# Order of the two column chunks of every expert: 2048 then 1536 columns, or 1536 then 2048

## What is computed

```python
D_MODEL = 1024; D_FF = 7 * D_MODEL // 2      # 3584
def swiglu(x, wg, wu, wd):
    return (jax.nn.silu(x @ wg) * (x @ wu)) @ wd

logits = (xt @ w_router).astype(jnp.float32)
top_v, top_i = lax.top_k(logits, TOP_K)      # 2 of 8
w = jax.nn.softmax(top_v, axis=-1)
gates = jnp.sum(jax.nn.one_hot(top_i, N_EXPERTS) * w[..., None], axis=1)
for e in range(N_EXPERTS):
    y = y + gates[:, e:e + 1] * swiglu(xt, wg[e], wu[e], wd[e])
```

## Time and profile before

| | us |
|---|---|
| median of 3 runs | 1382.66 (1381.82 to 1394.2) |
| profiled execution, its own time | 1382.52 |
| its span, first to last instruction | 1380.8 |
| TensorE busy | 1329.7 (96%) |
| VectorE, ScalarE, GpSimd busy | 746.8, 643.1, 35.4 |

### The profile page before, as it was taken

The page is one execution under the profiler, slowest core; times in us unless marked ns, Lnnn a source line. Parts: engine busy times, 40 slices in busy tenths (PEclk is TensorE's granted clock), DMA queues, the critical chain, the costliest instruction groups (busy, mean ns, idle before and its releaser), DMA issues.

```text
span 1380.8 us, 16480 instructions
## 1 busy us (share of the span) xinstructions
PE 1329.7 (96%) x6528; PEld 947.1 (69%) x6528; DVE 746.8 (54%) x787; ACT 643.1 (47%) x751; POOL 35.4 (3%) x96
## 2 busy tenths in 40 slices
PE   7999999999999999999999999999989999989994
PEld 6877788888878777658468558478448568538561
DVE  4646644445455567547358357268247358327443
ACT  5465433444354646347157147157137147236341
POOL 2000000000000000000000000000000000000001
PEclk9999999999999999999999999999999999999998
DMA  9730855554535459899999999999999999999995
GB/s 334 252 138 1 305 183 185 189 194 164 183 101 179 153 209 347 321 421 388 418 422 421 421 420 419 417 421 422 422 420 418 419 420 422 422 421 418 419 419 226
DMA packets 102031, 444.38 MB, mean 322 GB/s; under 512 B 9982, under 2 KB 22140, under 8 KB 71228
## 3 DMA queue, kind: packets, MB, share of 16 engines
q1 hardware_dynamic: 100388, 438.24, 80.5%
q0 software_dynamic: 1440, 4.98, 0.9%
q10 hardware_dynamic: 120, 0.04, 0.0%
HBM read 439.30 MB, written 3.93 MB: 321 GB/s over the span
## 4 chain that ended last, share of the span: by engine, by line
PE 85%; DMA 6%; ACT 4%; DVE 3%; issue 1%; POOL 0%; DVEq 0%; POOLq 0%; ACTq 0%; SPq 0%
PE bank L915 81%; PE bank L918 3%; DMA part_in<-in_moe_w_down_dram 2%; DMA more<-in_moe_w_down_dram 2%; DMA ring<-in_moe_w_down_dram 2%; ACT part_h L1577 1%; DVE ring_l L1980 1%; ACT xn L1577 0%; DVE part_l L1980 0%; DVE nmax L2187 0%; ACT prob L1769 0%; ACT sg L1902 0%; ACT pxh L1577 0%; ACT in_h L1577 0%; ACT L1742 0%
## 5 line engine op out<-in xcount | busy, mean ns | idle before, releaser
L1577 ACT ACTIVATE part_h<-ring 128x2048 fp32r<-128x2048 f32 (+1 forms) x122 | 221.5, 1820 | 140.8 <-PE bank L915 118.6
L915 PE MATMUL bank<-part_h,xh 128*128 128x512 f32 x688 | 271.4, 394 | 4.9 <-ACT sg L1902 2.1
L915 PE MATMUL bank<-part_h,xl 128*128 128x512 f32 x688 | 268.6, 390 | 0.0
L1980 DVE TENSOR_TENSOR ring_l<-ring,part_h 128x2048 fp32r<-128x2048 f32 (+1 forms) x80 | 167.6, 2105 | 73.5 <-ACT part_h L1577 73.3
L915 PEld LDWEIGHTS bank<-part_h,xh 128*128 128x128 f32 x688 | 129.3, 188 | 36.4 <-issue 7.3
L915 PEld LDWEIGHTS bank<-part_h,xl 128*128 128x128 f32 x688 | 129.2, 188 | 27.4
L1980 DVE TENSOR_TENSOR part_l<-ring,part_h 128x2048 fp32r<-128x2048 f32 x42 | 96.1, 2292 | 80.6 <-ACT part_h L1577 80.6
L915 PE MATMUL bank<-part_h,hTh 128*128 128x512 f32 x320 | 127.7, 399 | 11.7 <-DVE ring_l L1980 6.4
L915 PE MATMUL bank<-part_l,xh 128*128 128x512 f32 x333 | 129.7, 390 | 0.0
L1980 DVE TENSOR_TENSOR hTl<-bank,hTh 128x512 fp32r<-128x512 f32 x40 | 27.1, 690 | 183.4 <-ACT hTh L1577 183.4
L915 PE MATMUL bank<-part_h,hTl 128*128 128x512 f32 x320 | 125.9, 394 | 0.0
(11 more groups left out here) (390 smaller groups left out, 2043.5 us busy)
## 6 DMA issues: line engine op xcount, KB each, us to landing
ring<-in_moe_w_down_dram SPq DMA_DIRECT2D x48, 1024.0 KB, 16.7
ring<-in_moe_w_up_dram SPq DMA_DIRECT2D x32, 1024.0 KB, 17.7
ring<-in_moe_w_gate_dram SPq DMA_DIRECT2D x23, 1024.0 KB, 21.5
part_in<-in_moe_w_down_dram SPq DMA_DIRECT2D x23, 1024.0 KB, 16.4
ring<-in_moe_w_gate_dram SPq DMA_DIRECT2D x30, 768.0 KB, 16.6
ring<-in_moe_w_up_dram SPq DMA_DIRECT2D x25, 768.0 KB, 17.3
ring<-in_w_in_dram SPq DMA_DIRECT2D x7, 2048.0 KB, 8.8
ring<-in_dense_w_gate_dram SPq DMA_DIRECT2D x14, 1024.0 KB, 5.1
```

What stands on the lines that cost most here:

```text
L915: return nc.tensor.matmul(o, lhsT, rhs, start=start, stop=stop)
L1577: return nc.scalar.activation(dst, src, ACT.Copy, scale=scale)
L1980: return nc.vector.tensor_tensor(o, a, b, op)
```

## The change

`CHUNKS` gives the same two sizes in the other order, and with them their start columns: before [(0, 2048), (2048, 1536)], after [(0, 1536), (1536, 2048)].

```diff
     CHUNK = 4 * W
-    CHUNKS = [(c, min(CHUNK, FF - c)) for c in range(0, FF, CHUNK)]
+    CHUNKS = [(max(c - CHUNK, 0), min(CHUNK, c)) for c in range(FF % CHUNK, FF + 1, CHUNK)]
     QUARTERS = CHUNK // W
```

## The result

| | before | after |
|---|---|---|
| median of 22 runs each, us | 1383.26 (1380.18 to 1394.81) | 1389.7 (1387.68 to 1400.28) |
| ratio | | 1.0057, interval 1.0039 to 1.0076 |
| span of the profiled execution, us | 1380.8 | 1387.6 |

The changed kernel is slower: by 0.57% by the ratio, by 6.4 us (0.46%) between the medians, and by 6.8 us between the two profiled spans. That is within the 1% that the prediction took as no change, but the interval excludes 1. In both kernels some runs are 10 us longer than the rest; those of the changed kernel have a mean granted clock of 0.98 instead of 0.99. The forecast was 1387.0, in a range of 1380 to 1394.

What follows compares the result with a forecast made beforehand. The prediction took the weight stream, held by full slots through step 0 and again at 630 to 652 us, as the bound. Its terms +7.2 - 2.6 + 0.4 - 0.5 = +4.5 us on 1382.5 gave 1387.0 us, range 1380 to 1394.

Steps and rivals of the forecast that it cites:

- What bounds the kernel: Whole kernel: the weight stream's last landing sets the end, then 17.8 us of tail, though TensorE is 96% busy.
- Part two: Step 0, to piece 29: 7.5 MiB more left to land, +18.7 us, less 11.5 us for its earlier landing, +7.2 us.
- Part four: Gather and SiLU hand-overs in step 0: less work covers them, bound 0 to +1.4 us, taken as +0.4 us.
- Part three: Stream held a second time, 630 to 652 us, at 372 GB/s: this goes after the change, -2.6 us.
- a hold at step 4: Small pieces ahead again at step 4: 9.5 us queued, 4 us of room, taken as 0, bound 0 to +2 us.
- Part one: Before the first product: 14 slots hold 10.5 MiB instead of 14; the 3.5 MiB left cost 8.7 us of stream.
- One sign in the list of what would show it: Step 0, 526.7 to 566 us: if the forecast is right, the stream's GB/s stays about as before (319).
- Part five: Last windows: 2.4 us of idle DMA engines, perhaps from `fetch` arriving late; up to -2.4 us, taken as -0.5 us.
- No difference: Rival, chance 0.11: TensorE, 96% busy, sets the end and the stream catches up; 1382.5 us.
- Faster: Rival, chance 0.07: late start absorbed, hold at 630 to 652 us and idle engines at the end gone; 1377.5 us.
- Clearly slower by TensorE's waits: Rival, chance 0.06: waits before wide down pieces and a lower clock, 7.2 us each in three pairs; 1409 us.

Runs made afterwards that it cites:

- less_tensor_work: Kernel before without the third of three products in gate and up pieces of steps 8 and 12; 1382.1 us in one run, last landing 0.0.
- late_prefetch: Kernel before with pieces 11, 12 and 13 held back until piece 0 is used; 1382.82 us in one run, last landing +0.7 us.
- w0_short_first: Kernel before with only expert place 0 taking its 1536-column chunk first; 1380.83 us beside 1381.77, ratio 0.9998 (0.997 to 1.0026).
- n1_short_first: Kernel before with only place 1, the first narrow expert, taking its 1536-column chunk first; 1388.08 us beside 1381.77, ratio 1.0039 (1.0019 to 1.006).
- small_fetch: Changed kernel with each of four fetches of parked rows cut to a plain load of 64 of 1024 columns; 1383.9 us in one run.
- pair0_short_first: Kernel before with places 0 and 1 taking their 1536-column chunks first, the other six 2048 first; 1387.57 us in one run, last landing +6.5 us.
- early_table: Kernel before with a one-column SiLU on ScalarE after the split of piece 5, loading the activation table early; 1381.12 us beside 1382.23, ratio 1.0003.

## Why the prediction was right, and where not

**What bounds the kernel: right.** less_tensor_work takes 29 us of matmuls away and moves the last landing by 0.0.

**Part two, the sum by bytes at piece 29: right in kind, one size off.** The terms can be measured one by one. From 652 us on both kernels load at 420 GB/s, so 7.5 MiB are the +18.7 us of the prediction. Piece 29 goes out earlier by 50.68 - 41.18 = 9.5 us (predicted 10.9, less the 0.4 of part four) and lands quicker by 5.1 - 4.3 = 0.8 (predicted 0.6). The fit that this part quotes from the Trainium skill, page "DMA: Bandwidth & Descriptors", stands there in the section "Anatomy of one DMA — SWDGE (gpsimd) path" and is for DMAs issued by GpSimd; these pieces are issued by SyncE. No term of the sum rests on it.

**Part four, the hand-overs of step 0: 1.4 us, not 0.4.** The pieces alone do give 10.9, so 1.4 is given back. The issue rows show where. Piece 16 goes out 8.60 us after the start before and 7.26 after, 0.7 short of the 2.04 of three shorter pieces. The pieces around the SiLUs lose 0.3 more and the piece after the gather the 0.4 that was predicted. The 0.7 is a hand-over that the prediction doesn't have: VectorE has small operations to do and begins the split of the third piece (`spare_l`) 2.94 us after the start in both kernels. Before, TensorE is busy with the first two pieces until that split is done; after, it is through with them earlier and waits. Two rows of each kernel, before and then after:

```profile
529.62 2.29 DVE L1980 TENSOR_TENSOR spare_l<-spare,part_h 128x2048 fp32r<-128x2048 f32 x1
532.21 0.39 PE L915 MATMUL bank<-part_h,xh 128*128 128x512 f32 x1
```

```profile
529.38 1.75 DVE L1980 TENSOR_TENSOR spare_l<-spare,part_h 128x1536 fp32r<-128x1536 f32 x1
531.18 0.50 PE L915 MATMUL bank<-part_h,xh 128*128 128x512 f32 x1 [0.38 <-DVE spare_l L1980]
```

**Part three, the second hold: right in kind and size.** It went: 423 for 372 GB/s, and 22 us x 51/420 are 2.7 us, against 2.6 predicted. The fear of a hold at step 4 was needless: 12.8 us are queued there.

**Part one, "That is the cost": wrong.** The 3.5 MiB less in the prefetch are the step that failed in the reasoning, though they didn't enter the sum. late_prefetch loses 3 MiB and nothing of the time, and w0_short_first has the small prefetch and no loss. The cost lies one stage later, in what fills the slots that come free during step 0: the gate and up pieces of step 1. That was in part two's count (30 x 0.75) and not in the words. One sign in the list of what would show it failed for the same reason: from 526.7 to 566 us the changed kernel loads at 282 GB/s, where the kernel before had 334 (the prediction's 319 is that of the window to 577.4). In this window n1_short_first has 270 and w0_short_first 355.

**Part five, the end: wrong in its reason.** I took -0.5 for engines idle because of `fetch`. small_fetch shows that the idle stays without it. In these two profiles it even grew, from 10 x (1 - 312/420) = 2.6 us to 10 x (1 - 253/420) = 4.0, so +1.4. The last 10 us before the last landing, before and then after:

```profile
1354.71:1364.71 10.00, 5.48 (x24) 1.26 (x20) 3.05 (x3) 0.00 (x0) 0.00 (x0) 1.00 0.77 312
1361.51:1371.51 10.00, 5.81 (x24) 1.45 (x24) 2.71 (x4) 0.00 (x0) 0.00 (x0) 1.00 0.61 253
```

That the change causes this isn't shown: with the last three pairs as before the same time lies between 1.5 and 3.8.

**The sum.** +18.7 - 9.5 - 0.8 - 2.7 + 1.4 = +7.1, and measured +7.0. The forecast +4.5 lacks 2.5: 1.0 from part four and 1.9 from the end, less 0.2 for the landing and 0.1 for the hold; the 0.1 left over is rounding. Worked out in the same way, the other kernels come out within 0.5 us. n1_short_first: 3.5 MiB are +8.7, the landing -0.8 (that of the changed kernel; its own isn't in the trace), the hold -2.6, the end +1.2, together +6.5 (measured +6.7). pair0_short_first: +18.7 - 9.4 - 0.8 - 2.6 + 0.6 = +6.5 (+6.5). early_table: -1.4 for piece 29, -0.6 for the hold (383 instead of 372 GB/s), -0.3 for the end, together -2.3 (-2.0). w0_short_first: +10.0 - 9.4 - 2.6 + 0.3 = -1.7 (-1.2); there the stream is no longer held at piece 29, which lands 7.2 us after its issue, so the formula fits less well.

**The rivals.** "No difference" fell with the ratio's interval. "Faster" needed a rate well under 420 somewhere after 650 us, and up to the last 10 us there was none. "Clearly slower by TensorE's waits": TensorE waited on `ring_l` splits for 11.0 instead of 7.4 us and at most 6.1 us at once, and the stream took no notice, as less_tensor_work explains. Here the waits of an engine that isn't the bound cost nothing.

The rows of TensorE's waits in the expert stage of the changed kernel:

```profile
PE bank L915 <- DVE ring_l L1980: 11.0, 5, 6.1
PE bank L915 <- DVE part_l L1980: 5.7, 2, 5.2
```

## What to carry to other kernels

Where a load stream sets the end, find the last moment at which it is held back, and count what has landed by then: in this kernel that moment and those bytes counted, and how much was prefetched before it didn't. A ring of slots that each hold one piece of any size is worth the bytes that it holds at that moment, so the pieces next in line should fill their slots. And work on the "bound" engine may be worth one for one before the hold ends and nothing after it. Before an account of single microseconds is believed, each term needs a measurement of its own: here 1.4 us of the difference between two profiles lie in the last 10 us, which scatter as much from kernel to kernel.

## What the runs showed of the hardware that I had not expected

The 16 DMA engines don't end a long stream together: in small_fetch, with almost nothing but weights in the queues, the mean share falls over the last six us (0.71, 0.60, 0.48), while the last landings still come every 2.5 us (TensorE's last down pieces begin at 1363.67 and 1366.14). In all thirteen profiles the idle time in the last 10 us is between 1.5 and 4.0 us. A reading that would fit is that each landing waits for the engine that is furthest behind, so that the stream's rate at the end is that engine's. It isn't shown: the traces that were kept don't tell the single engines apart.

```profile
1363.67 1.94 PE L913 MATMUL bank<-spare,hTn 128*64 128x512 f32 x8 [0.52 <-DMA spare<-in_moe_w_down_dram]
1366.14 1.94 PE L913 MATMUL bank<-more,hTn 128*64 128x512 f32 x8 [0.53 <-DMA more<-in_moe_w_down_dram]
```
